# A third seven-product step in the gate-and-up loop, its weight sums on GpSimd, and the first forms kept in another buffer

## The reference, cut to what matters

```
hf  = rmsnorm(x, norm_ffn)                      # 256 x 2048
act = silu(hf @ w_gate) * (hf @ w_up)           # w_gate, w_up: 2048 x 5632
x   = x + act @ w_down                          # w_down: 5632 x 2048
out = rmsnorm(x, norm_final)
```

## Time and profile before

| | before |
|---|---|
| runs, median of 3 (lowest, highest) | 1755.92 us (1755.33, 1756.76) |
| profiled execution | 1755.32 us, of it span 1753.5 us |
| TensorE busy | 1732.6 us, 99% |
| VectorE busy | 995.3 us, 57% |
| ScalarE busy | 794.2 us, 45% |
| GpSimd busy | 173.3 us, 10% |
| mean granted TensorE clock | 0.997 |
| DMA | 331.09 MB, mean 189 GB/s |

### The profile page before, as it was taken

One profiled execution on the slowest core, in us unless ns is written; L12 is line 12 of the kernel. 1 busy time (PEld: TensorE's weight loads), 2 busy tenths in 40 slices (PEclk: granted clock), 3 DMA queues, 4 the chain that ended last, 5 costly groups with the idle time before them and its releaser, 6 DMA issues.

```text
span 1753.5 us, 21136 instructions
## 1 busy us (share of the span) xinstructions
PE 1732.6 (99%) x7817; PEld 1434.9 (82%) x7817; DVE 995.3 (57%) x749; ACT 794.2 (45%) x706; POOL 173.3 (10%) x109
## 2 busy tenths in 40 slices
PE   9999999999999999999999989999999999999997
PEld 7888888888888888888888868888888888888886
DVE  5454455556565545444445466777777777544445
ACT  6444444445454433333334545444444445444444
POOL 1000010100000000000000023222322221000000
PEclk9999999999999999999999999999999999999999
DMA  8656655555555555655556545555555555555552
GB/s 288 194 171 191 190 164 174 168 167 180 165 182 192 194 193 190 194 189 193 190 192 216 192 148 203 198 194 191 192 195 197 198 198 195 213 191 191 191 193 94
DMA packets 152106, 331.09 MB, mean 189 GB/s; under 512 B 8736, under 2 KB 8832, under 8 KB 146048
## 3 DMA queue, kind: packets, MB, share of 16 engines
q1 hardware_dynamic: 152064, 330.51, 56.6%
HBM read 328.38 MB, written 2.10 MB: 188 GB/s over the span
## 4 chain that ended last, share of the span: by engine, by line
PE 96%; DVE 1%; POOL 1%; ACT 1%; issue 0%; DMA 0%; SPq 0%; DVEq 0%; POOLq 0%; ACTq 0%
PE ps L1342 18%; PE ps L1343 18%; PE ps L1351 18%; PE ps L1619 9%; PE ps L1620 9%; PE ps L1624 9%; PE ps L1689 4%; PE ps L1696 4%; PE ps L1691 4%; PE ps L1360 1%; PE ps L1580 1%; ACT w_hi L499 0%; DVE w_lo L884 0%; POOL t_raw L477 0%; DMA w_raw<-in_w_in 0%
## 5 line engine op out<-in xcount | busy, mean ns | idle before, releaser
L884 DVE TENSOR_TENSOR w_lo<-w_raw,w_hi 128x2048 fp32r<-128x2048 f32 x308 | 732.8, 2381 | 500.9 <-ACT w_hi L499 498.9
L499 ACT ACTIVATE w_hi<-w_raw 128x2048 fp32r<-128x2048 f32 (+1 forms) x309 | 589.5, 1911 | 447.3 <-PE ps L1343 214.0
L1342 PE MATMUL ps<-w_hi,xT_hi 128*128 128x512 f32 x1024 | 404.5, 395 | 0.9 <-ACT w_hi L499 0.9
L1343 PE MATMUL ps<-w_hi,xT_lo 128*128 128x512 f32 x1024 | 398.7, 389 | 0.0
L1351 PE MATMUL ps<-w_lo,xT_hi 128*128 128x512 f32 x1024 | 253.0, 389 | 0.0
L1342 PEld LDWEIGHTS ps<-w_hi,xT_hi 128*128 128x128 f32 x1024 | 192.3, 188 | 41.1 <-ACT w_hi L499 1.1
L1351 PEld LDWEIGHTS ps<-w_lo,xT_hi 128*128 128x128 f32 x1024 | 192.2, 188 | 39.9
L1343 PEld LDWEIGHTS ps<-w_hi,xT_lo 128*128 128x128 f32 x1024 | 192.4, 188 | 39.0
L1619 PE MATMUL ps<-w_hi,fT_hi 128*128 128x512 f32 x440 | 173.8, 395 | 7.6 <-DVE w_lo L884 7.3
L1620 PE MATMUL ps<-w_hi,fT_lo 128*128 128x512 f32 x440 | 171.7, 390 | 0.0
L477 POOL TENSOR_TENSOR t_raw<-w_raw 128x1024 f32<-128x1024 f32 x22 | 56.1, 2552 | 821.4 <-DVE form_lo L1197 532.8
(11 more groups left out here) (220 smaller groups left out, 1728.7 us busy)
## 6 DMA issues: line engine op xcount, KB each, us to landing
w_raw<-in_w_in SPq DMA_DIRECT2D x127, 1024.0 KB, 5.5
w_raw<-in_w_gate SPq DMA_DIRECT2D x88, 512.0 KB, 3.6
w_raw<-in_w_up SPq DMA_DIRECT2D x88, 512.0 KB, 4.4
w_raw<-in_w_down SPq DMA_DIRECT2D x44, 1024.0 KB, 4.8
w_raw<-in_w_branch_a SPq DMA_DIRECT2D x16, 1024.0 KB, 5.1
w_raw<-in_w_branch_b SPq DMA_DIRECT2D x16, 1024.0 KB, 5.0
w_raw<-in_w_out SPq DMA_DIRECT2D x16, 1024.0 KB, 5.1
xn<-in_x SPq DMA_DIRECT2D x4, 512.0 KB, 8.4
```

The costliest lines, as they stand in the source:

```text
L499: copy = lambda o, i, **kw: nc.scalar.activation(o, i, ACT.Copy, **kw)
L884: V.tensor_tensor(w_lo[:, chunk.split, :], w_raw[:, chunk.raw, :], w_hi[:, chunk.split, :].bitcast(F32), ALU.subtract).then_inc(lo_split, 1)
L1342: T.matmul(ps[:, banks + r, :], rows(hi, k, r), w, start=(q == 0 and k == 0), stop=False)
L1343: last = T.matmul(ps[:, banks + r, :], rows(lo, k, r), w, start=False, stop=False)
```

## The change

It makes position 5 of each turn an S step too (`STEPS = "SssSsSss"`), swaps the pairs of positions 4 and 5 so that the new S step takes pair 4, and moves `LAST_S` from 3 to 5: the three banks that only S steps write (P1, P6, P7) are now emptied after step 5. Form group 1 gets one pair with sums (two more forms). GpSimd makes the weight sums of positions 0, 3 and 5. `form_raw0` moves from over `t_raw` to over `t_lo`; GpSimd's wait for `form_lo` before the first weight sums goes, and VectorE has it before the first `t_lo` instead.

```diff
-STEPS = "SssSssss"
-PAIR_OF = (0, 2, 3, 1, 4, 5, 6, 7)
-LAST_S = 3
+STEPS = "SssSsSss"
+PAIR_OF = (0, 2, 3, 1, 5, 4, 6, 7)
+LAST_S = 5
...
-        FORMS = 20
+        FORMS = 22
...
-        form_raw0 = at("form_raw0", [P, 12, P], F32, s + 2 * HALF_CH)
+        form_raw0 = at("form_raw0", [P, 12, P], F32, s + HALF_CH)
...
-        form_raw1 = at("form_raw1", [P, 8, P], F32, Z)
+        form_raw1 = at("form_raw1", [P, 10, P], F32, Z)
...
-        FORM_STEPS = (0, 5, 7)
+        FORM_STEPS = (0, 5, 10)
...
-                if starts(i) and j == 0:
-                    pool.wait_ge(form_lo_done, 1)
-                else:
+                if not (starts(i) and j == 0):
                     pool.wait_ge(t_lo_done, before)
...
-            weight_sums(LAST_S, 0)
+            for j in (3, LAST_S):
+                weight_sums(j, 0)
             with pool.Fori(1, FB) as i:
-                for j in (0, LAST_S):
+                for j in (0, 3, LAST_S):
                     weight_sums(j, i)
...
-                        forms_high(1, form_raw1, 12, 8)
+                        forms_high(1, form_raw1, 12, 10)
...
-                    if last and j == LAST_S + 2:
+                    if last and j == LAST_S + 1:
                         stage(Chunk(G_DOWN))
...
                 before = S_BEFORE[j] + i * S_TURNS
+                if starts(i) and j == 0:
+                    dve.wait_ge(form_lo_done, 1)
                 dve.wait_ge(t_hi_done, before + 1)
...
-                        forms(1, form_raw1, KB)
+                        forms(1, form_raw1, KB - 1)
...
-                        forms_low(1, form_raw1, 12, 8)
+                        forms_low(1, form_raw1, 12, 10)
...
-                plain = (2, 4)[g]
+                plain = (2, 3)[g]
```

## The result

The changed kernel takes 1769.3 us (median of 3 runs, 1769.2 to 1769.53) against 1755.92 us: 1.0078 times the time before, 95% interval 1.0062 to 1.0094. It is slower by 13.4 us, where 20 us (1776 against 1755.92) was forecast. One of the ten executions of one experiment's kernel, the one with the low split of step 6 cut, took 5105 us at a granted clock of 1.00 and is left out of its interval.

The account below looks back on a forecast made before the run. TensorE, 99% busy, bounds the kernel now; the change makes a chain through GpSimd's sums decide. Head and turn 0 -0.3, nine turns +20.7, last turn +0.6: +21.0 on 1755.32, 1776 us; range 1762 to 1789.

Parts of the forecast that it names:

- The matmuls removed: Step 5 has 21 matmuls instead of 24: 33 fewer over 11 turns, 7.5 us, 0.68 us a turn.
- The chain: Sums of 5 wait for t_lo of 3, next step 0's for t_lo of 5: +2.0 us a turn.
- ripple at step 1's low part: VectorE's additions begin later, so w_lo of 1 is ready at about 8.7, wanted at 8.4: +0.3 us.
- +2.3 us a turn: Turns 1 to 9: +2.0 us from the late next step 0 plus 0.3 us at step 1, 20.7 us.
- the price of an insertion: Each w_lo that becomes ready during a set of GpSimd sums lengthens it by about 2.2 us.
- the third rival: GpSimd's first addition beats w_lo of 5, step 5's low half waits 1.6 us: 1788 us, chance 0.08.
- The head: First sums start near 998, TensorE 6.4 us earlier; together with turn 0 -0.3 us, bounds -7.8 and +4.
- The last turn: No next step 0: stall 1.0 plus 0.3 at step 1 minus 0.68 for fewer matmuls, +0.6 us.
- The clock: At the loop's head, 0.77 over 1026 to 1032 after the long idle; 1.4 us counted as saved.
- the sums stay hidden: The GpSimd chain fits if five waits for VectorE cost under 8.3 us a turn: 1740 us, chance 0.14.
- One insertion fewer: One w_lo fewer holds the sums of 5 or next 0: turn about 43.0 us, 1750 to 1758, chance 0.10.
- The handover: A blocked GpSimd operation starts some 115 ns after VectorE's ends: 0.6 us a turn, 1781 us, 1 in 20.

Follow-up runs that it names:

- the kernel with the step alone: Changed kernel with form_raw0 back over t_raw and GpSimd's wait for form_lo back, leaving only the third S step: 1778.33 us, 1.0127.
- the last versions: Changed kernel with sums of 5 on VectorE (1744.16 us) or t_hi of 3 earlier (1748.17); with turn 0's sums of 3 earlier, 1741.77 and 1746.27.
- the kernel with narrow sums: Changed kernel with the weight sums of position 5 cut to 16 of 512 columns: 1742.91 us, 0.9925.

## Why the prediction was right, and where its sizes were off

**The matmuls removed** came out as stated, and 42.45 us is what a turn takes wherever nothing waits (sums of 5 cut, on VectorE, or anchored earlier: 42.44 us).

**The chain** is right in every link, in times from the start of step 0 at 1158.47:

| | forecast | measured |
|---|---|---|
| `t_lo` of 3 ends | 14.7 | 14.8 |
| sums of 5 released `t_hi` | 24.3 | 24.3 |
| step 5 starts | 27.65 | 27.75 |
| sums of next 0 released `t_hi` | 39.3 | 38.9 |
| next step 0 starts | 45.1 | 44.9 |
| ripple at step 1's low part | +0.3 | none |

The forecast by execution was +21.0 us and the profiled one has +13.9, so 7.1 us too much. The term mis-sized is "+2.3 us a turn", which measured +1.77 (1068.66 to 1472.71 are nine turns of 44.89, against 43.13): 9 x 0.53 = 4.8 us of the overshoot. 0.3 us a turn of it is the ripple: VectorE's two multiplications took 2.98 us instead of 3.33, and `w_lo` of 1 was ready at about 7.8, not 8.7. The rest, 0.2 us a turn, is the price of an insertion, taken as 2.2 us where the five measured 1.94 to 2.15 (the additions' lengths less 2.40 or 1.29), less what went the other way: the last sums began at 27.7 and not 27.6, and from their `t_hi` to step 0 it took 5.95 us and not 5.76. The 0.3 us that step 7 was to wait did not appear either.

The path also hung on a close race. In this turn the `w_lo` of 5 started at 1186.13 and GpSimd's first addition is shown from 1186.16; the two were as close in each of the nine turns, and `w_lo` was first each time. Had the addition been first, the third rival (step 5's low half late, 1788 us) would have had its condition. That it went the forecast's way was in part luck: the text put the two within 0.1 us and gave the other outcome a chance of 0.08, without a reason for the order.

**The head** I put at -0.3 us together with turn 0. TensorE entered at 1018.91, not 1019.3, and GpSimd's first sums began at 998.57 as said; step 3 started at 1037.96 (forecast 1038.5), step 5 at 1051.64, 13.7 us later (forecast 14.7), and turn 1 at 1068.66 (forecast 1070.8). The kernel before starts its turn 1 at 1070.95 (the text's 1071.1 is a slip: 1157.20 - 2 x 43.13 is 1070.94), so head and turn 0 measured -2.3 us. The 2.0 us between lie within the bounds given for turn 0. How far its order can swing is seen in the kernel with the step alone, where GpSimd was held for 5.5 us instead of 2 at the same place.

**The last turn** and what follows cost 0.3 us (+0.6 forecast; the ripple is missing here too): -2.3 + 9 x 1.77 + 0.3 = 13.9 us, the difference of the spans.

**The clock** did not fall before turn 0: the wait of 0.45 us left it at 1.00 over 1018 to 1026, where the earlier trace rows had 0.77 for the first step. The 21 matmuls of step 0 took 4.88 us (1018.91 to 1023.79) instead of 6.28 (1025.76 to 1032.04), so the 1.4 us that the text counts as saved were saved.

**The rivals.** That the sums stay hidden (1740 us) fell by the order, not by the amount, of work: its time is what the last versions reach. *One insertion fewer* did not happen: all five were there in each of the nine turns. The kernel with `w_lo` of 6 cut has two fewer and took 1755.5 us, near the 1754 that the text gave for one. The handover of the page "SBUF — State Buffer" of the Trainium skill, "A bandwidth-pool intuition that's wrong (but worth ruling out)", with some 115 ns behind each hold, was not seen. (The page measured it on a transfer whose descriptors GpSimd writes, behind a VectorE copy, and not on additions.) In the kernel with narrow sums a 32-column addition held from 1164.54 ended at 1166.92, 0.13 us after the `w_lo` that held it (1166.79), and such a one takes at least 0.22 us by itself:

```profile
1164.54 2.38 POOL L476 TENSOR_TENSOR t_raw<-w_raw 128x32 f32<-128x32 f32 x1 [9.78 <-DVE t_lo L1167]
1166.99 0.22 POOL L479 TENSOR_TENSOR w_raw<-t_raw,w_raw 128x16 f32<-128x16 f32 x1
```

```profile
1164.50 2.29 DVE L884 TENSOR_TENSOR w_lo<-w_raw,w_hi 128x2048 fp32r<-128x2048 f32 x1
```

The same page's section "SBUF: two separate sides" calls the pair of ports that VectorE and GpSimd share an exclusive lock, held for a whole instruction; the holds of turn 3, 1.94 to 2.15 us each beside subtractions of 2.29 us, are of that kind, but the three subtractions in a row show that GpSimd, once it waits, does not get in at each instruction's end.

## What to carry to other kernels

When work goes to an engine that the profile calls 10% busy, add up the chain in which its results stand, in the program's order, and count into each GpSimd operation every VectorE subtraction of two SBUF tiles that becomes ready while the set runs: 5 us of additions took 11.1 us here (1186.16 to 1197.29). Then look for the chain's anchor: one ScalarE instruction made earlier, with the same work on all engines, turned the changed kernel from 0.8% slower to 0.5% faster. And run the parts of a change apart; here 5.7 us of gain lay hidden under 22.3 us of loss.

## What the runs showed that I had not expected

GpSimd can be held over three VectorE instructions in a row (7.92 us for an addition of 2.4 us), although in nearly all other places it got in after the first. In the changed kernel the same three subtractions met the same addition and one of them was made to wait (`form_lo`, 3.67 us). The next VectorE instruction was ready 1.6 us before the end of the running one in the first case and 1.2 us in the second; in the steady turns, where GpSimd got in, 0.5 us. That alone cannot decide: at the end of `form_lo` in the first case the next one, `w_lo` of 4, had also been ready for 1.2 us, and GpSimd did not get in. What decides was not tried and stays open.

The sums of 512 columns take 0.69 us on VectorE and 1.28 us on GpSimd, those of 1024 columns 1.22 and 2.40 us, where nothing holds them. VectorE, at 57% the busier engine, was the cheaper place for the third set.
